# Output stage of a decoder layer: from channel rows to token rows, on one core

## The chip, the cores and the metric

The kernel runs on one core of a Trainium2 chip. The metric is the device time of one execution in microseconds, from runs of one program; lower is better. Engines are named as the profile names them: PE (TensorE, matmul; PEld is its weight load), DVE (VectorE), ACT (ScalarE), POOL (GpSimd), SP (SyncE), which issues most DMAs here. An ending q (SPq, PEq) is an engine's own queue of instructions. Values are fp32; the large products are made from split fp32r operands.

## The reference

One decoder layer over 1024 tokens with a model width of 1024: a half-step feed-forward block, a mixer (gated DeltaNet beside differential attention, merged by gates), a second feed-forward block, and a last RMSNorm. The change concerns the last line and the row of weights it needs:

```
def rms_norm(x, g, eps=RMS_EPS):                  # RMS_EPS = 1e-6
    y = x * rsqrt(mean(x * x, axis=-1) + eps)
    return y * g

x = x + 0.5 * swiglu_ffn(rms_norm(x, ffn2_norm), ffn2_w_gate, ffn2_w_up, ffn2_w_down)
return rms_norm(x, final_norm)                    # (1, 1024, 1024) float32
```

## The kernel before, in words

The stream x lives in SBUF as xT, transposed: 128 partitions by 8 chunks of channels by 1024 tokens, so that channel c sits on partition c mod 128 and the matmuls can contract over channels. Work is cut into phases (setup, feed-forward, five mixer phases, feed-forward, output). Each phase is one block with a program for each engine, ordered by semaphores that are waited for by hand; `end_phase` clears them and puts a barrier of all engines between phases (lines 86 to 90). There is no planner: the order on an engine is the order of its lines, and a wait holds up all that stands behind it on that engine.

**Setup** (`setup_phase`, line 119). SP loads four gain vectors into one tile, `gains` (lines 149 to 153), each spread over partitions in pieces of 4 bytes, and after them the rows of x, 128 tokens (512 KB) at a time into two slots (lines 154 to 157; a slot is loaded again once PE has transposed what it held). PE transposes each, DVE copies the result to xT (line 204). ACT's queue loads small mixer parameters at the same time (lines 601 to 613). The setup ends with a wait for all gains.

**Feed-forward** (`ffn_phase`, line 342). It ends with PE's last down product and `add_down` on DVE (line 472), which adds each chunk to xT.

**Output** (`output_phase`, line 281) uses the class `Norm` (line 209), as the other norms do, on the transposed x, where the sum over channels runs across partitions:
- ACT squares the eight chunks (line 227); DVE adds them in pairs (line 244).
- PE multiplies the four pair sums by a matrix of ones (line 251), which leaves the sum of squares of each token on all 128 partitions.
- ACT takes the root of 128 by 1024 (line 231), DVE its reciprocal (line 258), and then eight products of a chunk with its column of gains and the reciprocals (line 261).
- PE waits for all eight (`pe.wait_ge(norm.scaled, DC)`, line 311), then transposes token tile by token tile, two groups of four into four PSUM banks (line 317).
- DVE copies the even group of a tile (line 330), ACT the odd one (line 306), into one of two row tiles; SP stores it, 512 KB (line 337). From the third tile on both copies wait for the store that used the slot before.

Lines of other phases that the prediction uses for durations: 774 (a copy from PSUM on ACT), 1327 (the softmax's exp with a row sum), 1381 (a product with a pointer scalar and one input in PSUM), 1387 to 1398 (the one- and two-column operations behind the softmax), 766 (the root in the DeltaNet projection, with its table load), 616 and 618 (small exponentials in the setup).

Of the kernel before, what the change touches and what calls it, by code (L numbers as in the profile page):

```python
# [118 lines left out]
def setup_phase(core, a):  # L119

    nc = core.nc
    c = core
    per = core.ctx
    c.xT = c.sb(per, "xT", [P, DC, T])
    c.n_hi = c.sb(per, "n_hi", [P, DC, T], F32R)
    c.n_lo, c.n_raw = c.sb_shared(per, "n_lo", [P, DC, T])
    c.ident = c.sb(per, "ident", [P, P])
    c.ones = c.sb(per, "ones", [P, P])
    c.head_ones = c.sb(per, "head_ones", [P, P])
    c.ident2 = c.sb(per, "ident2", [P, CH])  # L130
    c.gains = c.sb(per, "gains", [P, 4, DC])
    c.eps = c.sb(per, "eps", [P, 2])

    gains_in = c.sem("gains_loaded")
    zeroed = c.sem("consts_zeroed")
    made = c.sem("consts_made")
    turned = c.sem("x_turned")
    taken = c.sem("x_taken")
    with ExitStack() as ctx:
        mixer_part = mixer_setup(core, a, ctx)  # L140
        xin = c.sb(ctx, "x_in", [P, 2, D_MODEL])
        xps = c.ps(ctx, "x_ps", [P, 4, HALF])
        slot_in = [c.sem("x_in_slot0"), c.sem("x_in_slot1")]
        block = ctx.enter_context(nc.Block())
        xrows = a["x"].rearrange("b (t p) d -> (b t) p d", p=P)

        @block.sync
        def _(sp):
            for i, name in enumerate(("ffn1_norm", "mix_norm", "ffn2_norm")):
                sp.dma_start(c.gains[:, i, :], a[name].rearrange("l (c p) -> p (l c)", p=P),  # L150
                             allow_slow_non_contiguous=True).then_inc(gains_in, 16)
            sp.dma_start(c.gains[:, 3, :], a["final_norm"].rearrange("(c p) -> p c", p=P),
                             allow_slow_non_contiguous=True).then_inc(gains_in, 16)
            for t in range(T // P):
                if t >= 2:
                    sp.wait_ge(turned, 2 * (t - 1))
                sp.dma_start(xin[:, t % 2, :], xrows[t]).then_inc(slot_in[t % 2], 16)
            sp.wait_ge(gains_in, 64)

        @block.gpsimd  # L160
        def _(pool):
            pool.memset(c.ident[:], 0.0).then_inc(zeroed, 1)
            pool.memset(c.ones[:], 1.0).then_inc(zeroed, 1)
            pool.memset(c.eps[:, 0:1], RMS_EPS).then_inc(zeroed, 1)
            pool.memset(c.eps[:, 1:2], SUBLN_EPS).then_inc(zeroed, 1)
            pool.memset(c.head_ones[:], 0.0).then_inc(zeroed, 1)
            pool.wait_ge(zeroed, 5)
            pool.affine_select(out=c.ident[:], in_=c.ident[:], compare_op=ALU.not_equal, fill=1.0, base=0,
                               pattern=[[-1, P]], channel_multiplier=1).then_inc(made, 1)
            mixer_part["gpsimd"](pool)  # L170

        @block.scalar
        def _(act):
            mixer_part["scalar"](act)

        @block.tensor
        def _(pe):
            pe.wait_ge(made, 1)
            for t in range(T // P):
                pe.wait_ge(slot_in[t % 2], 16 * (t // 2 + 1))  # L180
                for g in range(2):
                    k = 2 * t + g
                    if k >= 4:
                        pe.wait_ge(taken, k - 3)
                    for j in range(4):
                        d = 4 * g + j
                        last = pe.transpose(xps[:, k % 4, j * P:(j + 1) * P],
                                            xin[:, t % 2, d * P:(d + 1) * P], c.ident[:])
                    last.then_inc(turned, 1)
            mixer_part["tensor"](pe)  # L190

        @block.vector
        def _(dve):
            mixer_part["clear"](dve)
            dve.wait_ge(zeroed, 5)
            for h in range(2):
                dve.memset(c.head_ones[h * HD:(h + 1) * HD, h * HD:(h + 1) * HD], 1.0)
            dve.wait_ge(made, 1)
            dve.tensor_tensor(c.ident2[:], c.ident[:, 0:CH], c.ident[:, CH:P], ALU.add)
            for t in range(T // P):  # L200
                for g in range(2):
                    k = 2 * t + g
                    dve.wait_ge(turned, k + 1)
                    dve.tensor_copy(c.xT[:, 4 * g:4 * g + 4, t * P:(t + 1) * P],
                                    xps[:, k % 4, :].rearrange("p (j q) -> p j q", j=4)).then_inc(taken, 1)
            mixer_part["vector"](dve)


class Norm:
# [1 line left out]

    def __init__(self, core, which, rstd, ss, split=True):
        self.core, self.gain, self.rstd, self.ss, self.split = core, core.gains[:, which, :], rstd, ss, split
        self.squared = core.sem("squared")
        self.paired = core.sem("squares_paired")
        self.summed = core.sem("squares_summed")
        self.rooted = core.sem("rooted")
        self.inverted = core.sem("inverted")  # L220
        self.scaled = core.sem("scaled")
        self.hi_made = core.sem("n_hi_made")
        self.lo_made = [core.sem("n_lo_even_made"), core.sem("n_lo_odd_made")]
# [31 lines left out]
    def scale(self, dve):  # L255
# [4 lines left out]
        for k in range(DC):  # L260
            dve.scalar_tensor_tensor(out=c.n_raw[:, k, :], in0=c.xT[:, k, :], scalar=self.gain[:, k:k + 1],  # L261
                                     in1=self.rstd[:], op0=ALU.mult, op1=ALU.mult).then_inc(self.scaled, 1)
            if self.split and k % 2:
                self.lo_part(dve, k - 1)

    def lo_part(self, engine, k):
# [11 lines left out]
        pe.wait_ge(self.lo_made[k % 2], k // 2 + 1)  # L278


def output_phase(core, which, out):

    nc, c = core.nc, core
    turned = c.sem("y_turned")
    copied = c.sem("y_copied_even")
    copied_act = c.sem("y_copied_odd")
    with ExitStack() as ctx:
        rstd = c.sb(ctx, "rstd", [P, T])
        ss = c.ps(ctx, "ss", [P, NH, HALF])
        y = c.sb(ctx, "y", [P, 2, D_MODEL])  # L290
        yps = c.ps(ctx, "yps", [P, 4, HALF])
        slot_out = [c.sem("y_out0"), c.sem("y_out1")]
        norm = Norm(c, which, rstd, ss[:], split=False)
        block = ctx.enter_context(nc.Block())
        orow = out.rearrange("b (t p) d -> (b t) p d", p=P)

        @block.scalar
        def _(act):
            norm.squares(act)
            norm.root(act)  # L300
            for t in range(T // P):
                k = 2 * t + 1
                if t >= 2:
                    act.wait_ge(slot_out[t % 2], 16 * (t // 2))
                act.wait_ge(turned, k + 1)
                act.activation(y[:, t % 2, HALF:], yps[:, k % 4, :], ACT.Copy).then_inc(copied_act, 1)  # L306

        @block.tensor
        def _(pe):
            norm.sums(pe)  # L310
            pe.wait_ge(norm.scaled, DC)
            for t in range(T // P):
                for g in range(2):
                    k = 2 * t + g
                    past(pe, (copied, copied_act)[g], t - 1)
                    for j in range(4):
                        last = pe.transpose(yps[:, k % 4, j * P:(j + 1) * P],  # L317
                                            c.n_raw[:, 4 * g + j, t * P:(t + 1) * P], c.ident[:])
                    last.then_inc(turned, 1)

        @block.vector
        def _(dve):
            norm.pairs(dve)
            norm.scale(dve)
            for t in range(T // P):
                k = 2 * t
                if t >= 2:
                    dve.wait_ge(slot_out[t % 2], 16 * (t // 2))
                dve.wait_ge(turned, k + 1)
                dve.tensor_copy(y[:, t % 2, 0:HALF], yps[:, k % 4, :]).then_inc(copied, 1)  # L330

        @block.sync
        def _(sp):
            for t in range(T // P):
                sp.wait_ge(copied, t + 1)
                sp.wait_ge(copied_act, t + 1)  # L336
                sp.dma_start(orow[t], y[:, t % 2, :]).then_inc(slot_out[t % 2], 16)
            sp.wait_ge(slot_out[0], 16 * (T // P // 2))
            sp.wait_ge(slot_out[1], 16 * (T // P // 2))


def ffn_phase(core, which, w_gate, w_up, w_down):
# [1462 lines left out]
def build(nc, a, out):  # L1805
    with ExitStack() as ctx:
# [5 lines left out]
        mixer(core, a)  # L1812
        ffn_phase(core, 2, a["ffn2_w_gate"], a["ffn2_w_up"], a["ffn2_w_down"])
        core.end_phase()
        output_phase(core, 3, out)
        core.end_phase()


# [22 lines left out]
```

## Time and profile before

| | |
|---|---|
| median of 3 runs | 2977.3 us |
| lowest, highest | 2975.35, 2978.68 us |
| span of the profiled execution | 2974.8 us |
| its own time | not given by the profile; the span runs from its first to its last instruction |
| PE busy | 2670.5 us (90%), 17130 instructions |
| PE weight load | 2164.7 us (73%) |
| DVE busy | 1292.1 us (43%), 1443 instructions |
| ACT busy | 636.3 us (21%), 852 instructions |
| SP's DMA queue (q1) | 109.15 MB, 12.3% of 16 engines |
| mean granted clock of PE | 0.941 of full speed |

The page gives busy time over the whole span. The output stage lies inside the last fortieth of it, so its own state is read from the chain of waits, from the timeline and from windows cut around it. Times in such rows count from the start of the span. A row of the timeline gives start, length, engine, line, operation and tiles, the count of merged instructions, and in square brackets how long the engine sat idle before and what released it; a row without brackets followed at once. [...]

### The profile page before, as it was taken

The numbers are of one execution on the slowest core, as the hardware profiler recorded it, in microseconds if no ns is written. First come the engines' busy times: TensorE is split into PE (matmuls) and PEld (weight loads), VectorE is DVE, ScalarE is ACT, GpSimd is POOL, SyncE is SP. The second block draws the span as 40 slices with busy tenths as digits, with TensorE's granted clock in tenths as the row PEclk, the third lists the DMA queues.
The fourth block names the chain that finished last, engine by engine and source line by source line (L and its number), as shares of the span: only waits on it lengthen the run. The fifth ranks groups of instructions, "written<-read, shape, count | busy, mean of one in ns | idle before, by whom it ended". The sixth has DMA issues, their size and how long they took to land. (4 is left out here: it accounts for less than half of the span.)

```text
span 2974.8 us, 40256 instructions
## 1 busy us (share of the span) xinstructions
PE 2670.5 (90%) x17130; PEld 2164.7 (73%) x17130; DVE 1292.1 (43%) x1443; ACT 636.3 (21%) x852; POOL 72.8 (2%) x88
## 2 busy tenths in 40 slices
PE   4999999999789778777888698999969999999995
PEld 3888888888557677776666456888748888888874
DVE  6333333333478744443455542444363333333334
ACT  2111111111255211111333331111131111111111
POOL 2000000000010000000000000000010000000000
PEclk7999999999899888788999889999999999999997
DMA  3111111111110000001100001111011111111101
GB/s 85 50 57 50 49 49 44 48 42 49 29 29 28 1 3 3 3 3 37 29 22 1 15 15 57 46 47 49 28 57 50 47 45 49 42 56 45 48 27 57
DMA packets 167517, 110.97 MB, mean 37 GB/s; under 512 B 15336, under 2 KB 158696, under 8 KB 167400
## 3 DMA queue, kind: packets, MB, share of 16 engines
q1 hardware_dynamic: 160720, 109.15, 12.3%
q8 instruction: 102, 1.67, 0.2%
q10 hardware_dynamic: 6680, 0.03, 0.1%
q14 instruction: 15, 0.12, 0.0%
HBM read 104.97 MB, written 4.19 MB: 37 GB/s over the span
## 5 line engine op out<-in xcount | busy, mean ns | idle before, releaser
L472 DVE SCALAR_TENSOR_TENSOR xT<-ps_down,xT 128x1024 f32<-128x1024 f32 x176 | 215.6, 1225 | 247.5 <-PE ps_down L100 247.5
L455 DVE TENSOR_TENSOR w_lo<-w_raw,w_hi 128x1024 fp32r<-128x1024 f32 x132 | 163.6, 1253 | 352.5 <-ACT w_hi L409 352.5
L409 ACT ACTIVATE w_hi<-w_raw 128x1024 fp32r<-128x1024 f32 x132 | 136.9, 1053 | 745.1 <-PE ps_down L100 395.7
L96 PE MATMUL ps_gate<-n_hi,w_hi 128*128 128x512 f32 x704 | 220.8, 395 | 35.7 <-DVE n_lo_hi L269 25.1
L96 PE MATMUL ps_down<-h_hi,w_hi 128*128 128x512 f32 x704 | 218.2, 391 | 7.6 <-issue 7.6
L98 PE MATMUL ps_gate<-n_lo_hi,w_hi 128*128 128x512 f32 x704 | 218.5, 392 | 0.0
L100 PE MATMUL ps_gate<-n_hi,w_lo 128*128 128x512 f32 x704 | 218.1, 391 | 0.0
L98 PE MATMUL ps_down<-h_lo,w_hi 128*128 128x512 f32 x704 | 217.8, 391 | 0.0
L100 PE MATMUL ps_down<-h_hi,w_lo 128*128 128x512 f32 x704 | 217.6, 390 | 0.0
L98 PE MATMUL ps_up<-n_lo_hi,w_hi 128*128 128x512 f32 x704 | 216.7, 389 | 0.0
L96 PE MATMUL ps_up<-n_hi,w_hi 128*128 128x512 f32 x704 | 216.7, 389 | 0.0
L100 PE MATMUL ps_up<-n_hi,w_lo 128*128 128x512 f32 x704 | 216.7, 389 | 0.0
L461 DVE TENSOR_TENSOR h_raw<-silu_gate,ps_up 128x1024 f32<-128x1024 f32 x44 | 53.7, 1221 | 332.1 <-PE ps_up L100 332.1
L96 PEld LDWEIGHTS ps_gate<-n_hi,w_hi 128*128 128x128 f32 x704 | 132.0, 189 | 69.9 <-issue 24.7
L96 PEld LDWEIGHTS ps_down<-h_hi,w_hi 128*128 128x128 f32 x704 | 132.7, 189 | 35.8 <-issue 8.3
L98 PEld LDWEIGHTS ps_gate<-n_lo_hi,w_hi 128*128 128x128 f32 x704 | 133.5, 190 | 28.1
L100 PEld LDWEIGHTS ps_gate<-n_hi,w_lo 128*128 128x128 f32 x704 | 133.0, 189 | 28.0
L98 PEld LDWEIGHTS ps_down<-h_lo,w_hi 128*128 128x128 f32 x704 | 133.0, 189 | 27.8
L100 PEld LDWEIGHTS ps_down<-h_hi,w_lo 128*128 128x128 f32 x704 | 132.7, 188 | 27.7
L98 PEld LDWEIGHTS ps_up<-n_lo_hi,w_hi 128*128 128x128 f32 x704 | 132.1, 188 | 27.5
L96 PEld LDWEIGHTS ps_up<-n_hi,w_hi 128*128 128x128 f32 x704 | 132.1, 188 | 27.4
L100 PEld LDWEIGHTS ps_up<-n_hi,w_lo 128*128 128x128 f32 x704 | 132.1, 188 | 27.4
(303 smaller groups left out, 4104.9 us busy)
## 6 DMA issues: line engine op xcount, KB each, us to landing
w_raw<-in_ffn_w_gate SPq DMA_DIRECT2D x44, 512.0 KB, 3.7
w_raw<-in_ffn_w_up SPq DMA_DIRECT2D x44, 512.0 KB, 3.7
w_raw<-in_ffn_w_down SPq DMA_DIRECT2D x44, 512.0 KB, 3.6
w_raw<-in_w_in SPq DMA_DIRECT2D x44, 512.0 KB, 3.6
x_in<-in_x SPq DMA_DIRECT2D x8, 512.0 KB, 3.9
w_raw<-in_w_out SPq DMA_DIRECT2D x8, 512.0 KB, 3.5
y_out<-y SPq DMA_DIRECT2D x8, 512.0 KB, 2.6
w_raw<-in_w_branch_a SPq DMA_DIRECT2D x8, 256.0 KB, 3.0
```

The costliest lines, as they stand in the source:

```text
L96: pe.matmul(bank, w_hi, x_hi[:, h * HALF:(h + 1) * HALF], start=start, stop=False)
L98: pe.matmul(bank, w_hi, x_lo[:, h * HALF:(h + 1) * HALF], start=False, stop=False)
L100: last = pe.matmul(bank, w_lo, x_hi[:, h * HALF:(h + 1) * HALF], start=False, stop=stop)
L409: act.activation(ring.hi[:, slot(k)], ring.raw[:, slot(k)], ACT.Copy).then_inc(ring.hi_made, 1)
L455: dve.tensor_tensor(ring.lo[:, slot(k)], ring.raw[:, slot(k)], ring.hi[:, slot(k)].bitcast(F32), ALU.subtract).then_inc(ring.lo_made, 1)
L461: dve.tensor_tensor(h_raw[:, j, :], sg[:], ps_u[:].rearrange("p h t -> p (h t)"), ALU.mult).then_inc(h_made, 1)
L472: dve.scalar_tensor_tensor(out=c.xT[:, d, :], in0=ps_d[:, d % 2].rearrange("p h t -> p (h t)"), scalar=0.5, in1=c.xT[:, d, :], op0=ALU.mul ...
```

## The change

The output stage works on token rows. PE transposes xT as it stands, eight 128 by 128 pieces to a token tile, into one of four PSUM slots of 1024 columns (all eight banks). ACT squares a tile from PSUM and has the row sum accumulated in the same instruction, then takes the root of that one column; a one-column root at the head of the stage draws the table load there. DVE takes the reciprocal of the column and makes one product from PSUM: tile times column times a row tile of weights. SP loads the weight row, broadcast to 128 partitions, at the head of the stage, and stores each tile from one of four slots. The load of `final_norm` in the setup goes, `gains` keeps three columns, and `Norm` loses a flag that only the old stage used. The call becomes `output_phase(core, a, out)`.

```diff
--- before.py
+++ after.py
@@ -128,7 +128,7 @@
     c.ones = c.sb(per, "ones", [P, P])
     c.head_ones = c.sb(per, "head_ones", [P, P])
     c.ident2 = c.sb(per, "ident2", [P, CH])
-    c.gains = c.sb(per, "gains", [P, 4, DC])
+    c.gains = c.sb(per, "gains", [P, 3, DC])
     c.eps = c.sb(per, "eps", [P, 2])
 
     gains_in = c.sem("gains_loaded")
@@ -149,13 +149,11 @@
             for i, name in enumerate(("ffn1_norm", "mix_norm", "ffn2_norm")):
                 sp.dma_start(c.gains[:, i, :], a[name].rearrange("l (c p) -> p (l c)", p=P),
                              allow_slow_non_contiguous=True).then_inc(gains_in, 16)
-            sp.dma_start(c.gains[:, 3, :], a["final_norm"].rearrange("(c p) -> p c", p=P),
-                             allow_slow_non_contiguous=True).then_inc(gains_in, 16)
             for t in range(T // P):
                 if t >= 2:
                     sp.wait_ge(turned, 2 * (t - 1))
                 sp.dma_start(xin[:, t % 2, :], xrows[t]).then_inc(slot_in[t % 2], 16)
-            sp.wait_ge(gains_in, 64)
+            sp.wait_ge(gains_in, 48)
 
         @block.gpsimd
         def _(pool):
@@ -211,8 +209,8 @@
 
 
 
-    def __init__(self, core, which, rstd, ss, split=True):
-        self.core, self.gain, self.rstd, self.ss, self.split = core, core.gains[:, which, :], rstd, ss, split
+    def __init__(self, core, which, rstd, ss):
+        self.core, self.gain, self.rstd, self.ss = core, core.gains[:, which, :], rstd, ss
         self.squared = core.sem("squared")
         self.paired = core.sem("squares_paired")
         self.summed = core.sem("squares_summed")
@@ -260,7 +258,7 @@
         for k in range(DC):
             dve.scalar_tensor_tensor(out=c.n_raw[:, k, :], in0=c.xT[:, k, :], scalar=self.gain[:, k:k + 1],
                                      in1=self.rstd[:], op0=ALU.mult, op1=ALU.mult).then_inc(self.scaled, 1)
-            if self.split and k % 2:
+            if k % 2:
                 self.lo_part(dve, k - 1)
 
     def lo_part(self, engine, k):
@@ -278,65 +276,70 @@
         pe.wait_ge(self.lo_made[k % 2], k // 2 + 1)
 
 
-def output_phase(core, which, out):
+def output_phase(core, a, out):
 
     nc, c = core.nc, core
-    turned = c.sem("y_turned")
-    copied = c.sem("y_copied_even")
-    copied_act = c.sem("y_copied_odd")
+    NT = T // P
+    SLOTS = 4
     with ExitStack() as ctx:
-        rstd = c.sb(ctx, "rstd", [P, T])
-        ss = c.ps(ctx, "ss", [P, NH, HALF])
-        y = c.sb(ctx, "y", [P, 2, D_MODEL])
-        yps = c.ps(ctx, "yps", [P, 4, HALF])
-        slot_out = [c.sem("y_out0"), c.sem("y_out1")]
-        norm = Norm(c, which, rstd, ss[:], split=False)
+        gain = c.sb(ctx, "gain_rows", [P, D_MODEL])
+        y = c.sb(ctx, "y", [P, SLOTS, D_MODEL])
+        sq = c.sb(ctx, "y_squared", [P, D_MODEL])
+        ss = c.sb(ctx, "y_sums", [P, NT])
+        rstd = c.sb(ctx, "y_rstd", [P, NT])
+        yps = c.ps(ctx, "yps", [P, SLOTS, D_MODEL])
+        gain_in = c.sem("gain_in")
+        warm = c.sem("root_warm")
+        turned = c.sem("y_turned")
+        summed = c.sem("y_summed")
+        rooted = c.sem("y_rooted")
+        inverted = c.sem("y_inverted")
+        normed = c.sem("y_normed")
+        y_out = [c.sem(f"y_out{i}") for i in range(SLOTS)]
         block = ctx.enter_context(nc.Block())
         orow = out.rearrange("b (t p) d -> (b t) p d", p=P)
 
+        @block.tensor
+        def _(pe):
+            for t in range(NT):
+                past(pe, normed, t - SLOTS + 1)
+                for d in range(DC):
+                    last = pe.transpose(yps[:, t % SLOTS, d * P:(d + 1) * P], c.xT[:, d, t * P:(t + 1) * P],
+                                        c.ident[:])
+                last.then_inc(turned, 1)
+
         @block.scalar
         def _(act):
-            norm.squares(act)
-            norm.root(act)
-            for t in range(T // P):
-                k = 2 * t + 1
-                if t >= 2:
-                    act.wait_ge(slot_out[t % 2], 16 * (t // 2))
-                act.wait_ge(turned, k + 1)
-                act.activation(y[:, t % 2, HALF:], yps[:, k % 4, :], ACT.Copy).then_inc(copied_act, 1)
-
-        @block.tensor
-        def _(pe):
-            norm.sums(pe)
-            pe.wait_ge(norm.scaled, DC)
-            for t in range(T // P):
-                for g in range(2):
-                    k = 2 * t + g
-                    past(pe, (copied, copied_act)[g], t - 1)
-                    for j in range(4):
-                        last = pe.transpose(yps[:, k % 4, j * P:(j + 1) * P],
-                                            c.n_raw[:, 4 * g + j, t * P:(t + 1) * P], c.ident[:])
-                    last.then_inc(turned, 1)
+            act.activation(rstd[:, 0:1], c.eps[:, 0:1], ACT.Sqrt).then_inc(warm, 1)
+            act.wait_ge(warm, 1)
+            for t in range(NT):
+                act.wait_ge(turned, t + 1)
+                past(act, summed, t)
+                act.activation(sq[:], yps[:, t % SLOTS, :], ACT.Square, accum_out=ss[:, t:t + 1]).then_inc(summed, 1)
+                act.wait_ge(summed, t + 1)
+                act.activation(rstd[:, t:t + 1], ss[:, t:t + 1], ACT.Sqrt, scale=1.0 / D_MODEL,
+                               bias=c.eps[:, 0:1]).then_inc(rooted, 1)
 
         @block.vector
         def _(dve):
-            norm.pairs(dve)
-            norm.scale(dve)
-            for t in range(T // P):
-                k = 2 * t
-                if t >= 2:
-                    dve.wait_ge(slot_out[t % 2], 16 * (t // 2))
-                dve.wait_ge(turned, k + 1)
-                dve.tensor_copy(y[:, t % 2, 0:HALF], yps[:, k % 4, :]).then_inc(copied, 1)
+            dve.wait_ge(gain_in, 16)
+            for t in range(NT):
+                dve.wait_ge(rooted, t + 1)
+                dve.reciprocal(rstd[:, t:t + 1], rstd[:, t:t + 1]).then_inc(inverted, 1)
+                dve.wait_ge(inverted, t + 1)
+                if t >= SLOTS:
+                    dve.wait_ge(y_out[t % SLOTS], 16 * (t // SLOTS))
+                dve.scalar_tensor_tensor(out=y[:, t % SLOTS, :], in0=yps[:, t % SLOTS, :], scalar=rstd[:, t:t + 1],
+                                         in1=gain[:], op0=ALU.mult, op1=ALU.mult).then_inc(normed, 1)
 
         @block.sync
         def _(sp):
-            for t in range(T // P):
-                sp.wait_ge(copied, t + 1)
-                sp.wait_ge(copied_act, t + 1)
-                sp.dma_start(orow[t], y[:, t % 2, :]).then_inc(slot_out[t % 2], 16)
-            sp.wait_ge(slot_out[0], 16 * (T // P // 2))
-            sp.wait_ge(slot_out[1], 16 * (T // P // 2))
+            sp.dma_start(gain[:], a["final_norm"].unsqueeze(0).broadcast_to([P, D_MODEL])).then_inc(gain_in, 16)
+            for t in range(NT):
+                sp.wait_ge(normed, t + 1)
+                sp.dma_start(orow[t], y[:, t % SLOTS, :]).then_inc(y_out[t % SLOTS], 16)
+            for i in range(SLOTS):
+                sp.wait_ge(y_out[i], 16 * (NT // SLOTS))
 
 
 def ffn_phase(core, which, w_gate, w_up, w_down):
@@ -1812,7 +1815,7 @@
         mixer(core, a)
         ffn_phase(core, 2, a["ffn2_w_gate"], a["ffn2_w_up"], a["ffn2_w_down"])
         core.end_phase()
-        output_phase(core, 3, out)
+        output_phase(core, a, out)
         core.end_phase()
```

## Rows read from the trace of the kernel before

**Rows 1.** The page: its first line, and the queue of small packets.

```profile
span 2974.8 us, 40256 instructions
...
q10 hardware_dynamic: 6680, 0.03, 0.1%
```

**Rows 2.** The chain of waits, output stage: start us, us, what.

```profile
2926.50 2.01 ACT n_lo_raw L227 x2
...
2940.50 6.56 DVE rstd L258
...
2947.09 9.66 DVE n_lo_raw L261 x8
...
2956.79 3.69 PE yps L317 x16
...
2967.89 2.61 DMA y_out<-y
...
2970.52 0.69 DVE y L330
```

**Rows 3.** Timeline, the last addition of the feed-forward stage.

```profile
2924.43 1.23 DVE L472 SCALAR_TENSOR_TENSOR xT<-ps_down,xT 128x1024 f32<-128x1024 f32 x1 [1.49 <-PE ps_down L100]
```

**Rows 4.** Timeline, transposes of the setup, eight to a row.

```profile
14.68 1.09 PE L187 MATMUL x_ps<-ident,x_in 128*128 128x128 f32 x8 [2.13 <-DMA x_in<-in_x]
...
28.21 1.97 PE L187 MATMUL x_ps<-ident,x_in 128*128 128x128 f32 x8 [1.06 <-DMA x_in<-in_x]
```

**Rows 5.** Windows: us; PE, PEld, DVE, ACT, POOL busy; PEclk; DMA share; GB/s.

```profile
2924.00:2925.00 1.00, 0.39 (x2) 0.00 (x0) 0.57 (x1) 0.00 (x0) 0.00 (x0) 1.00 0.00 0
...
2927.00:2928.00 1.00, 0.00 (x0) 0.00 (x0) 0.00 (x0) 1.00 (x2) 0.00 (x0) 0.89 0.00 0
...
2956.00:2958.00 2.00, 1.21 (x6) 1.21 (x7) 0.79 (x2) 0.00 (x0) 0.00 (x0) 0.50 0.00 0
...
2962.00:2964.00 2.00, 1.98 (x17) 1.60 (x15) 0.87 (x2) 0.78 (x2) 0.00 (x0) 1.00 0.80 324
```

**Rows 6.** ACT: groups by form (busy us, mean ns), then timeline of a softmax.

```profile
L774 ACT ACTIVATE padded<-ps_proj 128x1024 f32<-128x1024 f32 x12 | 12.2, 1019 | 13.0 <-PE ps_proj L100 13.0
...
L231 ACT ACTIVATE rstd<-ss,eps 128x1024 f32<-128x1024 f32 x1 | 1.1, 1114 | 3.9 <-PE ss L251 3.9
...
L618 ACT ACTIVATE neg_a<-neg_a 16x1 f32<-16x1 f32 x1 | 0.2, 185 | 0.0
...
1640.45 1.14 ACT L1327 ACTIVATE scores<-scores,neg_max 128x1024 f32<-128x1024 f32 x1
1641.49 0.19 ACT L1327 ACTIVATION_READ_ACCUMULATOR scores<-scores,neg_max 128x1 f32 x1
1641.58 1.13 ACT L1327 ACTIVATE scores<-scores,neg_max 128x1024 f32<-128x1024 f32 x1
```

**Rows 7.** SP's waits (total, times, longest); landing times of the loads of x.

```profile
SPq L336 <- ACT y L306: 33.0, 1, 33.0
...
DMA to landing us min/median/max: 3.5/3.9/5.7
```

**Rows 8.** DVE: a product's group by form, then timeline in the attention stage.

```profile
L1381 DVE SCALAR_TENSOR_TENSOR scores<-bias,slopes,ps_scores 128x1024 f32<-128x1024 f32 x8 | 9.9, 1277 | 8.7 <-PE ps_turned L1246 8.7
...
1631.39 2.47 DVE L1381 SCALAR_TENSOR_TENSOR scores<-bias,slopes,ps_scores 128x1024 f32<-128x1024 f32 x2 [2.84 <-PE ps_turned L1246]
...
1645.34 0.16 DVE L1394 RECIPROCAL total<-total 128x2 f32<-128x2 f32 x1
1645.53 0.81 DVE L1396 TENSOR_SCALAR scores<-scores,total,neg_lam 128x1024 f32<-128x1024 f32 x1
```

**Rows 9.** Timeline of SP's queue in the setup.

```profile
2.55 1.21 SPq L152 DMA_DIRECT2D gains<-in_final_norm  x1
```

**Rows 10.** Timeline of ACT, a table load and its root.

```profile
868.37 1.28 ACT L766 ACT_TABLE_LOAD   x1
869.67 1.12 ACT L766 ACTIVATE root<-ps_sum,eps 128x1024 f32<-128x1024 f32 x1
```

## The prediction

> **What bounds the kernel now.** I read the page first: a span of 2974.8 us [rows 1], most of it PE's work in stages that the change does not touch. Such shares say nothing of the last stage, so I read the chain of waits next, which ended last there. From 2926.50 to the last copy at 2970.52 the stage is one serial chain [rows 2]: squares, pair sums, sums by matmul, root, reciprocal over 1024 columns (6.56), eight gain products (9.66), and only then, at 2956.79, transposition, copies and stores. The engines stand in a row here and each waits for the one before. The stage begins 0.84 us after the last add of the feed-forward stage (2925.66 to 2926.50), and its last copy ends at 2970.52 + 0.69 = 2971.21; behind it stand the last store and the closing, 2974.8 - 2971.21 = 3.6 us [rows 1 to 3]. In the store part two slots set the pace: a store lands 2.61 us after its issue, a copy of 0.69 follows, so two tiles take 3.3 us and the steps between, some 1.7 a tile [rows 2].
>
> **Part 1, the chain over channels goes.** All of 2926.50 to 2956.79, 30.3 us, is removed from the path, with the copies behind it. What takes its place is priced below from 2926.5 on, so the saving is the difference of the two ends of the last vector operation.
>
> **Part 2, the start.** PE can transpose as soon as the stage opens: x is complete and the identity is old. Eight transposes took 1.09 us at the full clock [rows 4], and 16 took 3.69 at the low one, 1.85 for eight [rows 2, 5]. PE enters at full clock (0.89 is the mean of 2927 to 2928 [rows 5]), so tile 0 is readable at about 2926.5 + 1.09 + 0.1 = 2927.7. ACT first loads the root table, 1.28, and does a one-column root. That root has a pointer bias: 128x1024 with one took 1114 ns and without one 1019, and a small one without took 185, so 0.28 [rows 6]. The first square starts at 2926.5 + 1.28 + 0.28 = 2928.1, behind tile 0. Before, that load lay under the sums; now it is open but cheap.
>
> The weight row comes by a DMA at the head of SP's queue in the stage. SP is in the stage at 2959.48 - 33.0 = 2926.45 [rows 7]. Nothing here shows a broadcast; the nearest is the load of x, the same 512 KB in rows of 4 KB into 128 partitions: 3.5 us at least, 3.9 median, 5.7 at most. Below it stands the store with 2.6. I take 3.5, since nothing else is in flight (the longer ones ran beside loads in small pieces): it lands at 2929.95, bounds 2929.05 and 2932.15. The vector engine waits for it ahead of all its work; behind that wait are all eight reciprocals, then PE from tile 4 (four slots) and the stores. Stores stand behind the load on SP for 0.33 us only, long before they are due. The squares run on meanwhile, up to the fourth slot.
>
> **Part 3, a tile on ACT.** Square with row sum, from PSUM: 1019 ns as the copy from PSUM; the read of the accumulator starts about 0.10 before its end and takes 0.19, as in the softmax (1640.45, 1641.49, 1641.58) [rows 6]. Sum ready at +1.11. Then the wait on its own result, 0.03 (no row on ACT; on the vector engine 1645.34 + 0.16 to 1645.53 [rows 8]), and the root, 0.28. The next square overlaps by 0.09: 1.33 a tile. Root of tile 0 at 2928.1 + 1.42 = 2929.5.
>
> **Part 4, a tile on the vector engine.** Reciprocal of one column: 0.158 for two columns; the product starts 0.20 after the reciprocal; product with pointer scalar and one input in PSUM 1.28; two such in a row took 2.47, so the next starts 1.19 after the first [rows 8]. 0.20 + 1.19 = 1.39, say 1.40 a tile. So the vector engine is the slowest of the chain, by little, and the end is: reciprocal 0 at 2929.98 (the weight row, 0.5 after root 0), + 7 x 1.40 + 1.48 = **2941.26**. Against 2971.21 that is 29.95 us less. If the weight row came at once, ACT would set it: 0.45 less. With 5.7 us of landing: 2.2 more.
>
> **Part 5, stores and slots.** A tile is stored every 1.40. A product from tile 4 on waits for the store issued 4 x 1.40 = 5.6 us less one product before, about 4.1, against 2.61 of landing: covered. With the queue busy the engines moved 324 GB/s at a share of 0.80 [rows 5], so 405 at a full one: 1.29 us for 512 KB, under 1.40. I leave the last landing and the closing at 3.6 us. Were these covers gone, the rival on stores has the price. The four slots of the transposes: tile t needs product t-4; PE (1.09) and ACT (1.33) then have 4.2 us. The work on PE and its weight loads lies beside.
>
> **Part 6, the setup.** One load in 4-byte pieces goes: 1.21 us of SP's queue ahead of the first load of x, from 2.55 on [rows 9]. PE's transposes in the setup wait for x [rows 4]. The stage is a chain of loads of x with two slots, so a shift of 1.21 should reach the end, but small loads from ACT's queue stay at their times and may eat part. Bounds 0 and 1.5; I take 0.9, nearer the issue time. The smaller gain tile moves the addresses behind it, at nothing: no row shows an address costing time, and its two bounds are the spread of the runs.
>
> **Sum.** 29.95 + 0.9 = 30.85. The profiled span is 2974.8; the execution's own time is not shown, and the median of the three runs, 2977.3, lies 2.5 above the span, which I leave as it is. 2977.3 - 30.85 = 2946.4 (a span of 2943.9).
>
> **Rivals.**
> A. *PE at the low clock for all tiles.* [...] A low clock for some tiles is in the forecast: tile 1 would come at 2929.5, covered by the weight row. Price if it stays: tile 7 at 2926.5 + 8 x 1.85 + 0.2 = 2941.5, + 1.11 + 0.31 + 0.20 + 1.28 + 0.05 = 2944.45, 3.2 more: 2949.6. Chance 0.08.
> B. *Stores set the pace.* If 324 GB/s is a ceiling and not the two slots' doing, a tile takes 1.62: first issue 2931.5, last landing 2931.5 + 7 x 1.62 + 2.61 = 2945.45 against 2943.9: 2948.0. Against it: the share of 0.80. Chance 0.10.
> C. *A table load at every change between square and root.* The change alternates them 8 times on ACT. The trace of before has a load ahead of each root and none ahead of a square, but nowhere does a square follow a root. Against: the squares that open this stage stand behind the silu of the feed-forward stage and begin without a load [rows 2], so they do not need the silu's loads; that they need none of the root's is not shown. Price by rows: a load takes 1.30 from its start to the next start [rows 10]; a tile takes 1.30 + 1.11 + 1.31 + 0.31 = 4.03, the last root is at 2928.1 + 8 x 4.03 = 2960.3, the last product ends at 2961.8, 9.4 less than before: 2977.3 - 9.4 - 0.9 = 2967.0. Chance 0.05.
> [...]
> D. *Slower: the broadcast goes in 4-byte pieces.* Place: the vector engine's first wait. The gain loads of before did so; 4 KB took 1.21 us of queue [rows 9], so 512 KB would take 128 x 1.21 = 155 us; by the share of the queue of small packets on the page, 0.1% of 2974.8 for 6680 packets [rows 1], 131072 packets take 58 us. The whole saving is gone when the row lands later than 3.5 + 30.85 = 34.4 us from issue; with 58 it lands at 2984.5, the time is 2977.3 + (2984.5 - 2929.95) - 30.85 = 3001, with 155 it is 3098. Against: source rows are contiguous over 4 KB as x's are, while the gains of before are spread over partitions. Chance 0.02.
> E. *The chain over channels was hidden.* Not possible by the chain of waits; that the text keeps one of its waits is not to be seen in the diff. Chance 0.01, 2977.
>
> **How the numbers follow.** Forecast 0.70, A 0.08, B 0.10, C 0.05, D 0.02, E 0.01, and 0.04 for something else between forecast and C. Predicted 2946.4. Its own bounds: down 0.45 (weight row), 0.6 (setup) and 1.95 for the spread of the runs (2977.3 - 2975.35), 3.0 together, 2943.4; up 2.2, 0.9 and 1.4: 2950.9. With A and B inside, the range is 2943.3 to 2951.5. A measurement tells 0.2% (6 us) from no change. Faster: 0.70 + 0.08 + 0.10 + 0.04 and 0.04 of C, 0.96; same: E, 0.01; slower: D, and 0.01 of C should a load cost 2.3 us and not 1.3, 0.03.
>
> **What would show it.** In the new profile: transposes from 2925.6 on (2926.5 less 0.9), one table load in the stage, squares near 1.02 with a 0.19 read, pitch of the products 1.40, the first product ended by the weight row and not by root 0, stores 2.6 to landing, no idle time of the vector engine before products from tile 4 on, 3.6 us from the last product to the end. Wrong: 16 loads (C), a pitch near 1.85 with clock 0.50 (A), a vector engine that waits for stores (B), a weight row over 6 us, or a setup that ends at the same time as before.

## The result, and the profile after

The changed kernel takes 2987.36 us (median of 13 runs, 2983.04 to 2990.72), the kernel before 2978.2 in the same comparison (13 runs, 2975.35 to 2982.36). The ratio is 1.003, 95% interval 1.0022 to 1.0039: slower by 0.3%, where 1% less was forecast. The profiled execution has a span of 2985.6 us, 10.8 more than before. Among the experiments below, one execution of the old stage with a wider tile took 14770 us, in the slow state, and is left out.

The chain of waits, output stage of the changed kernel (start us, us, what), answers to [rows 2]:

```profile
2967.45 3.29 DMA gain_rows<-in_final_norm
2970.74 0.02 issue
2970.77 0.18 DVE y_rstd L328
2970.94 0.03 issue
2970.97 1.28 DVE y L332
...
2980.69 1.28 DVE y L332
```

The stage opens at 2967.46 and its last product ends at 2980.69 + 1.28 = 2981.97: 14.51 us, where 44.71 stood before. The forecast stage was 2941.26 - 2926.5 = 14.8 us long; the change took 30.2 us out where 29.95 was forecast. But it opens 41 us later than before. Where from? The row of ACT with which each large stage begins, timeline of the changed kernel:

```profile
34.20 2.95 ACT L225 ACTIVATE n_lo_raw<-xT 128x1024 f32<-128x1024 f32 x3 [2.46 <-PEq L89]
...
810.14 5.79 ACT L225 ACTIVATE n_lo_raw<-xT 128x1024 f32<-128x1024 f32 x6 [28.12 <-PEq L89]
...
2191.81 4.84 ACT L225 ACTIVATE n_lo_raw<-xT 128x1024 f32<-128x1024 f32 x5 [16.24 <-PEq L89]
...
2967.46 1.28 ACT L313 ACT_TABLE_LOAD   x1 [28.09 <-PEq L89]
```

| stage | before | after |
|---|---|---|
| setup, to the first square | 34.43 | 34.20 |
| feed-forward 1 | 761.67 | 775.94 |
| mixer | 1370.22 | 1381.67 |
| feed-forward 2 | 760.18 | 775.65 |
| output, to the last product's or copy's end | 44.71 | 14.51 |

The starts before are 34.43, 796.10, 2166.32 and 2926.50; two of these rows, timeline of the kernel before:

```profile
796.10 4.84 ACT L227 ACTIVATE n_lo_raw<-xT 128x1024 f32<-128x1024 f32 x5 [27.11 <-PEq L89]
...
2166.32 3.90 ACT L227 ACTIVATE n_lo_raw<-xT 128x1024 f32<-128x1024 f32 x4 [16.41 <-PEq L89]
```

The three stages in the middle, which the change does not touch in any line of work, are 14.27 + 11.45 + 15.47 = 41.2 us longer; 41.2 - 30.2 - 0.2 = 10.8, the whole difference of the spans. The page shows on what engine: PE is busy for 2705.5 us against 2670.5.

The large products have this form. A chunk of weights is split into w_hi and w_lo, the normed x into n_hi and n_lo (the feed-forward's inner values into h_hi and h_lo). The function `three_pass` (from line 93 on) makes six matmuls of them, two halves of 512 tokens for each of three lines: w_hi with n_hi (L96), w_hi with n_lo (L98; the profile calls this tile n_lo_hi), w_lo with n_hi (L100). In the timeline each matmul has a weight load of its own (PEld, 128x128), which starts ahead of it and beside the matmul before: the first load of L98 starts at 2930.02 us, the first matmul of L98 at 2930.25, and the two of L96 take 2929.78 to 2930.41 (changed kernel, up product). n or h is the moving operand, the other input of the matmul's row, 128x512. The groups, page of the changed kernel (busy us, mean ns):

```profile
L98 PE MATMUL ps_up<-n_lo_hi,w_hi 128*128 128x512 f32 x704 | 221.3, 395 | 0.0
L96 PE MATMUL ps_up<-n_hi,w_hi 128*128 128x512 f32 x704 | 221.3, 395 | 0.0
L100 PE MATMUL ps_up<-n_hi,w_lo 128*128 128x512 f32 x704 | 221.3, 395 | 0.0
L96 PE MATMUL ps_down<-h_hi,w_hi 128*128 128x512 f32 x704 | 219.4, 393 | 7.5 <-issue 7.5
```

The first of them on the page of the kernel before:

```profile
L96 PE MATMUL ps_up<-n_hi,w_hi 128*128 128x512 f32 x704 | 216.7, 389 | 0.0
```

The up products had a mean of 389 ns each before and have 395 now; the down products, on the same weight tiles, 391 and 393. The timeline has it without the overlap of the modelled ends (changed kernel):

```profile
2926.98 0.63 PE L96 MATMUL ps_up<-n_hi,w_hi 128*128 128x512 f32 x2
2927.45 0.63 PE L98 MATMUL ps_up<-n_lo_hi,w_hi 128*128 128x512 f32 x2
2927.92 0.63 PE L100 MATMUL ps_up<-n_hi,w_lo 128*128 128x512 f32 x2
2928.38 0.63 PE L96 MATMUL ps_up<-n_hi,w_hi 128*128 128x512 f32 x2
...
2956.59 0.61 PE L100 MATMUL ps_down<-h_hi,w_lo 128*128 128x512 f32 x2
2957.04 0.62 PE L96 MATMUL ps_down<-h_hi,w_hi 128*128 128x512 f32 x2
2957.49 0.62 PE L98 MATMUL ps_down<-h_lo,w_hi 128*128 128x512 f32 x2
2957.95 0.61 PE L100 MATMUL ps_down<-h_hi,w_lo 128*128 128x512 f32 x2
```

Six up matmuls take 2928.38 - 2926.98 = 1.40 us from start to start, six down matmuls 2957.95 - 2956.59 = 1.36: 233.3 ns against 226.7 each. The granted clock is 1.00 in both stretches (PE busy 20.00 of 20.00 us in the window 2915 to 2935, 16.00 of 16.00 in 2948 to 2964), so it is not the clock. All products that move n_hi or n_lo are slow: 4224 in gate and up, 1152 in the projections of DeltaNet and attention, 192 in the branch norm and 768 in the merge. These are 6336, by 6.67 ns 42.2 us. (The expectations below count 6144, without the branch norm.)

PE's idle time does not grow: over the three stages in the middle it is busy for 2635.3 of 2892.1 us before and for 2683.1 of 2933.3 now. Each of these matmuls is 3% slower. That 42.2 lies so near to the 41.2 by which the stages are longer is in part chance: another part of the mixer is 3.6 us shorter (last section), so some 2.6 us more have no source named here.

### The profile page after: what moved, and what is told of

Same layout as the page of the kernel before. It is cut to its first block and busy times, and to the rows that moved or that the text cites. A ratio compares the mean times of both kernels' runs of the same rounds, so it can differ in the third digit from the quotient of the medians.

```text
span 2985.6 us, 40221 instructions
## 1 busy us (share of the span) xinstructions
PE 2705.5 (91%) x17114; PEld 2160.5 (72%) x17114; DVE 1275.7 (43%) x1438; ACT 633.0 (21%) x860; POOL 72.7 (2%) x88
## 5 line engine op out<-in xcount | busy, mean ns | idle before, releaser
L96 PE MATMUL ps_gate<-n_hi,w_hi 128*128 128x512 f32 x704 | 224.2, 399 | 37.3 <-DVE n_lo_hi L267 26.1
L96 PE MATMUL ps_down<-h_hi,w_hi 128*128 128x512 f32 x704 | 219.4, 393 | 7.5 <-issue 7.5
L100 PE MATMUL ps_gate<-n_hi,w_lo 128*128 128x512 f32 x704 | 222.1, 396 | 0.0
L98 PE MATMUL ps_gate<-n_lo_hi,w_hi 128*128 128x512 f32 x704 | 222.1, 396 | 0.0
L98 PE MATMUL ps_up<-n_lo_hi,w_hi 128*128 128x512 f32 x704 | 221.3, 395 | 0.0
L96 PE MATMUL ps_up<-n_hi,w_hi 128*128 128x512 f32 x704 | 221.3, 395 | 0.0
L100 PE MATMUL ps_up<-n_hi,w_lo 128*128 128x512 f32 x704 | 221.3, 395 | 0.0
L98 PE MATMUL ps_down<-h_lo,w_hi 128*128 128x512 f32 x704 | 218.8, 392 | 0.0
L100 PE MATMUL ps_down<-h_hi,w_lo 128*128 128x512 f32 x704 | 218.6, 392 | 0.0
L96 PEld LDWEIGHTS ps_gate<-n_hi,w_hi 128*128 128x128 f32 x704 | 131.5, 189 | 76.4 <-issue 24.7
L96 PEld LDWEIGHTS ps_down<-h_hi,w_hi 128*128 128x128 f32 x704 | 133.5, 190 | 36.5 <-issue 8.4
L98 PEld LDWEIGHTS ps_gate<-n_lo_hi,w_hi 128*128 128x128 f32 x704 | 132.5, 188 | 32.5
L100 PEld LDWEIGHTS ps_gate<-n_hi,w_lo 128*128 128x128 f32 x704 | 132.5, 188 | 32.5
L100 PEld LDWEIGHTS ps_up<-n_hi,w_lo 128*128 128x128 f32 x704 | 132.0, 187 | 32.3
L98 PEld LDWEIGHTS ps_up<-n_lo_hi,w_hi 128*128 128x128 f32 x704 | 132.0, 187 | 32.3
L96 PEld LDWEIGHTS ps_up<-n_hi,w_hi 128*128 128x128 f32 x704 | 132.0, 187 | 32.0
L98 PEld LDWEIGHTS ps_down<-h_lo,w_hi 128*128 128x128 f32 x704 | 133.3, 189 | 28.3
L100 PEld LDWEIGHTS ps_down<-h_hi,w_lo 128*128 128x128 f32 x704 | 133.3, 189 | 28.1
```

The lines of the kernel that those rows point to most:

```text
L96: pe.matmul(bank, w_hi, x_hi[:, h * HALF:(h + 1) * HALF], start=start, stop=False)
L98: pe.matmul(bank, w_hi, x_lo[:, h * HALF:(h + 1) * HALF], start=False, stop=False)
L100: last = pe.matmul(bank, w_lo, x_hi[:, h * HALF:(h + 1) * HALF], start=False, stop=stop)
```

## The experiments

Each time below is a median of four executions (ten for 128 bytes and for w_hi off, three for the old stage with a wider tile). Each ratio is to the kernel before in the same comparison, where that took 2976.7 to 2979.1 us; differences of 1 or 2 us between two experiments say nothing.

What n_hi and n_lo have to do with the change is not in its engines' programs. The gain tile went from 128 to 96 bytes a partition. Tiles are laid down one behind the other in the order of the kernel's calls: x, n_hi and n_lo ahead of the gain tile stayed, and all behind it (the weight ring, h_hi and h_lo, the mixer's tiles) moved down by 32 bytes. h and weights moved together, n and weights apart. That gave theory P: a matmul is slower when its weights and its moving operand lie at an unfavourable distance from each other. Against it stands theory Q: something else in the change slows PE.

### The tile restored

```diff
-    c.gains = c.sb(per, "gains", [P, 3, DC])
+    c.gains = c.sb(per, "gains", [P, 4, DC])
```

> The changed kernel, all of it, but the gain tile keeps four columns (128 bytes, the fourth unused), so every tile allocated behind it lies where it lay before the change. Theory P (placement: a matmul is slower when its weights and its moving operand start at places that differ by 32 bytes modulo 64): all products that move n_hi or n_lo return from 234 to 227 ns a matmul, the stages between setup and output take the 2892 us they took before, and the time is 2978.2 - 30.2 - 0.2 = 2947.8, 2945 to 2951. Theory Q (something else in the change slows PE: fewer DMAs in the setup, another set of semaphores, another program): 234 ns stay and the time stays near 2987.

Measured: 2947.57 us, ratio to before 0.9906 (0.9889 to 0.9922). By the same rows as above its feed-forward stages take 761.18 and 760.14, its mixer 1371.25; the up products are back (groups by form):

```profile
L96 PE MATMUL ps_up<-n_hi,w_hi 128*128 128x512 f32 x704 | 216.7, 389 | 0.0
```

Q falls. Every other part of the change is in this kernel, and 32 unused bytes are worth 40 us, four thirds of what the new output stage saves.

### The old stage with a wider tile

```diff
-    c.gains = c.sb(per, "gains", [P, 4, DC])
+    c.gains = c.sb(per, "gains", [P, 5, DC])
```

> The kernel before, nothing of the change, but the gain tile has five columns (160 bytes), so all behind it lies 32 bytes higher instead of 32 lower. Theory P: 6144 matmuls that move n_hi or n_lo take 6.7 ns more each, 41 us, 2978.2 + 41 = 3019, 3014 to 3024; the down products, whose two operands both move, stay at 227 ns. Theory Q: nothing, 2978.

Measured: 3019.46 us, ratio 1.0143 (1.0123 to 1.0164). The loss needs nothing of the change but the displacement, and either direction does.

### How far apart: 64, 128, 256 bytes

The changed kernel with `[P, 6, DC]`, `[P, 8, DC]` and `[P, 12, DC]`:

> The changed kernel with a gain tile of six columns (192 bytes): all behind it lies 64 bytes higher than before the change. Theory P with a period of 64 bytes: as with the tile restored, 2947.8 (2945 to 2951), 227 ns. With a period of 128 bytes or more the n products stay slow, near 234 ns, and the time near 2987. Theory Q: 2987.

> The changed kernel with a gain tile of eight columns, 256 bytes: all behind it lies 128 bytes higher than before the change. Theory P with a period of 128 bytes (64 was slow, 0 is not): 227 ns and 2947.6, 2945 to 2951. With a longer period: 233 ns in the n products, 2989. A shorter time than 2945 would mean that the old distance was not the best either.

> The changed kernel with a gain tile of 384 bytes: all behind it lies 256 bytes higher than before the change. In the kernel before every large product had its operands a multiple of 512 bytes apart; shifts of 32, 64 and 128 bytes were slow. Theory P with a period of 256: 227 ns and 2947.6, 2945 to 2951. With a period of 512: the n products near 233 ns and 2985 to 2990.

Measured: 2988.68 us for 64 bytes (ratio 1.0043, 1.0026 to 1.0059), 2985.46 for 128 (1.0029, 1.002 to 1.0039), 2947.12 for 256 (0.99, 0.9883 to 0.9916). My guesses of a period of 64 and of 128 were both wrong; the displacements seen to be fast are 0 and 256 bytes. Steps of 512 change nothing: within a stage the weights step by 512 bytes from chunk to chunk and the moving operand by 4096, and by 2048 from half to half, and in the kernel before the gap has a median of 227 ns in each large product. No profile shows a tile's address; that the operands lay a multiple of 512 bytes apart in the kernel before, as the last of these texts has it, was assumed, and no run shows it. The displacements count from the old places. Median gap from the start of one up matmul to the next, first and second of a pair, and the time (from the records of starts in each trace):

| displacement, bytes | n products: first, second ns | down products | us |
|---|---|---|---|
| 0 | 227, 227 | 227 | 2947.57 |
| -32 (the change) | 233, 234 | 227 | 2987.36 |
| +32 (old stage) | 232, 235 | 227 | 3019.46 |
| +64 | 233, 233 | 227 | 2988.68 |
| +128 | 238, 229 | 227 | 2985.46 |
| +256 | 227, 227 | 227 | 2947.12 |

The pair's mean is 233 to 233.5 wherever the products lose time: the pattern shifts, the sum does not. No displacement tried gave a faster n product than the old place. The time of +256 cannot be told from that of 0 (ratios 0.99 and 0.9906, with overlapping intervals).

### Distance or place

All 32 bytes off, the tile restored:

```diff
+    c.sb(per, "gap", [P, 8])
     c.xT = c.sb(per, "xT", [P, DC, T])
```

> The changed kernel with the tile restored and a gap of 32 bytes ahead of everything, so that every tile lies 32 bytes off, n and the weights alike. Theory P (only the distance between a matmul's moving operand and the weights modulo 128 bytes counts): 227 ns everywhere and 2947.6 as with the tile restored, 2945 to 2951. Theory R (each operand has to start at a multiple of 128 bytes): all large products slow, 6144 + some 2900 matmuls by 6.7 ns, 60 us, 3008.

Measured: 2948.39 us, ratio 0.9905 (0.9888 to 0.9922), 227 ns everywhere. R falls: with all operands 32 bytes off, each operand's own place has changed and nothing is slower; the distance between them matters.

The other pair of operands displaced, with n and weights in place:

```diff
         self.lo = core.sb(ctx, "w_lo", [P, depth, DC, P], F32R)
+        core.sb(ctx, "gap", [P, 8])
```

> The changed kernel with the tile restored and a gap of 32 bytes behind w_lo: the weights and n stay, what follows them (h_hi and h_lo in the feed-forward stages, merged_hi and merged_lo in the merge) lies 32 bytes off. Theory P: gate, up and projections stay at 227 ns, the down products (2112) and those of the merge's output (384) go to 233.5: 16.5 us over the tile restored, 2964, 2961 to 2968. A theory in which the writes of ACT and DVE, or a tile's own place, do the harm says that gate and up become slow too, as they did with the gap ahead of w_lo: near 2991.

Measured: 2965.4 us, ratio 0.9955 (0.9938 to 0.9971). Groups by form of this kernel, now with the roles exchanged:

```profile
L96 PE MATMUL ps_down<-h_hi,w_hi 128*128 128x512 f32 x704 | 224.0, 399 | 7.6 <-issue 7.6
...
L96 PE MATMUL ps_up<-n_hi,w_hi 128*128 128x512 f32 x704 | 217.1, 390 | 0.0
```

ACT and DVE write the displaced h here while gate and up run, and these stay fast. The changed kernel has a stretch that says the same: from 2929.20 to 2937.00 the up products run at 233.3 ns each while DVE, ACT and POOL are busy for 0.00 us and the DMA share is 0.00. No other engine is needed for the loss. What is left is PE's own work: in these 7.80 us its matmuls were busy for 7.75 and its weight loads for 5.88, beside them.

### Which two reads

> The changed kernel with the tile restored and a gap of 32 bytes between w_hi and w_lo, so w_lo and what follows (h_hi and h_lo among it) lie 32 bytes off, w_hi and n do not. It tells which pair of reads disturb each other. Theory P1 (the load of the next weights disturbs the matmul that runs meanwhile): in gate and up the second matmul of L98 and the first of L100 are slow, so the mean of both lines rises by 3.3 ns and L96 stays; in down (h off, w_hi not) both of L96, the first of L98 and the second of L100. Theory P2 (a matmul's own weights and its moving operand must agree): gate and up slow in L100 alone, both, by 6.7 ns; down slow in L96 and L98, fast in L100. Both give a third of 6144 and two thirds of some 2900 matmuls: 14 + 13 = 27 us over the restored tile, 2975, 2969 to 2980. Theory Q: no change against the restored tile.

> The changed kernel with the tile restored; in the two feed-forward stages w_hi alone lies 32 bytes off (a gap of 32 bytes ahead of it and one of 480 behind it, so w_lo and h lie 512 higher). Theory P1 (the next load disturbs the running matmul): of each six matmuls the four during which a w_hi is loaded are slow, L96 both, L98 first, L100 second; L98 second and L100 first stay at 227. Theory P2 (own weights and moving operand): L96 and L98 slow, L100 fast. Both: 4224 matmuls by 6.7 ns, 28 us over the tile restored, 2976, 2971 to 2981. If gate and up come out slow in all six, as with the gap ahead of w_lo, P1 is not the whole rule.

```diff
 # gap ahead of w_lo
         self.hi = core.sb(ctx, "w_hi", [P, depth, DC, P], F32R)
+        core.sb(ctx, "gap", [P, 8])
         self.lo = core.sb(ctx, "w_lo", [P, depth, DC, P], F32R)
 # w_hi off, feed-forward stages alone
+        core.sb(ctx, "gap", [P, 8])
         self.hi = core.sb(ctx, "w_hi", [P, depth, DC, P], F32R)
+        core.sb(ctx, "gap", [P, 120])
```

In their terms, P1 says that a running matmul is slowed by the load of the next weights, P2 that it is slowed by the place of its own weights. Measured: 2991.64 us (ratio 1.0049, 1.0032 to 1.0066) and 2982.26 (1.0013, 1.0004 to 1.0023), so 44 and 35 us over the restored tile and not 27 and 28. Median gaps in ns in the order of the six matmuls of a chunk; the last column is the median from the first start of one six to that of the next, so the rows need not add up to it:

| | L96 | L96 | L98 | L98 | L100 | L100 | all six |
|---|---|---|---|---|---|---|---|
| in place, all products | 227 | 227 | 227 | 227 | 227 | 227 | 1360 |
| gap ahead of w_lo, down | 233 | 234 | 231 | 227 | 227 | 235 | 1387 |
| gap ahead of w_lo, up | 233 | 231 | 232 | 235 | 231 | 231 | 1395 |
| w_hi off, gate, up and down | 231 | 229 | 235 | 232 | 231 | 235 | 1393 |

The down products of the first kernel are what P1 says, to the matmul: only the two during which an agreeing w_lo is loaded are fast. P2 would have made both of L98 slow and both of L100 fast. But its gate and up products, and all of the second kernel, are slow in every one of the six, which neither predicts: four agreeing loads in six (first kernel) or two (second) do not save their matmuls there. Shown is that the distance between moving operand and weights counts, and for the down products of the first kernel that it is the distance to the weights loaded during the matmul. Which load meets which matmul elsewhere, and why a misplaced one also costs its neighbours, stays open.

Operands in place do not rule out such gaps either. In the kernel before, behind sums that start every 429 ns (line 1474), the first products of the branch norm (from 1722.7 us on, granted clock 1.00) start 235, 233, 236, 224, 231, 236, 228, 233 and 231 ns apart and then settle to 226 and 227. Why they settle no run tested.

### A version to beat both

Weight row loaded during the last feed-forward stage, root table drawn at its end, x loaded ahead of the three gain vectors:

```diff
+        row = core.sb(ctx, "gain_row", [P, D_MODEL + P])   # first try: D_MODEL and a tile of 32
+        core.gain_row, core.root_first = row[:, 0:D_MODEL], row[:, D_MODEL:D_MODEL + 1]
...
+                act.activation(core.root_first, c.eps[:, 0:1], ACT.Sqrt)
...
+                sp.dma_start(c.gain_row, row.unsqueeze(0).broadcast_to([P, D_MODEL])).then_inc(row_in, 16)
```

> A version to beat both: the tile restored, the weight row loaded and the root table drawn during the last feed-forward stage, and the loads of x issued ahead of the three gain vectors in the setup. By the timeline of the changed kernel the first reciprocal stands 3.3 us behind the opening of the stage because of the weight row; without it the chain is transposes 1.2, square and its sum 1.11, root 0.3, so 2.65: 0.65 us less. The setup should give the queue time of three gain loads, 1.7 us at most, 0.5 by what the removal of the fourth gave. 2947.6 - 0.65 - 0.5 to 1.7 = 2945.9, 2943 to 2949; theory Q has no say in it.

Measured: 2958.44 us, ratio 0.9935 (0.9919 to 0.9952), 11 more than the restored tile. I had fallen into the same hole: 4096 + 128 bytes ahead of the ring of the last stage, 128 modulo 512. In its trace, last feed-forward stage:

```profile
L96 PE MATMUL ps_up<-n_hi,w_hi 128*128 128x512 f32 x352 | 110.7, 395 | 0.0
```

> The version with the weight row and the root table drawn early and x loaded first, now with the row tile 4608 bytes wide, 9 times 512, and not 4224: the weights of the last feed-forward stage keep their distance to n modulo 512. Theory P: the last feed-forward stage returns to 227 ns (it had 238 and 229 in turn) and the time falls from 2958.4 by 12.5 to some 2945.5; by the parts, 2947.6 less 0.85 in the output stage and 1.3 to 2.3 in the setup: 2945.0, 2942 to 2948. Theory Q, that the early loads themselves slowed that stage: it stays near 2958.

Measured: 2944.44 us, ratio 0.9887 (0.9871 to 0.9904), and the same group:

```profile
L96 PE MATMUL ps_up<-n_hi,w_hi 128*128 128x512 f32 x352 | 108.4, 389 | 0.0
```

This is the lowest median, though its interval overlaps that of the restored tile; the trace shows what it has over it: the first square of feed-forward 1 at 31.09 and not 33.57 us, and 0.4 in the output stage (PE's first transpose at 2924.97, last product ended at 2937.80 + 1.28 = 2939.08: 14.1, against 14.5).

## Why the prediction was wrong

**The step that failed** stands in part 6: "The smaller gain tile moves the addresses behind it, at nothing: no row shows an address costing time". The trace before had next to nothing to show: within a stage the operands of the large products change their distance by multiples of 512 bytes alone, from chunk to chunk and from half to half, and all ran at a median of 227 ns. The one other case in the same form is 48 small products of the DeltaNet projection, with weights of 16 columns laid 64 bytes apart. The last of them, from 840.89 us on, start 238, 234, 235, 229, 233 and 233 ns apart; but they are few and stand behind waits, and the large products right behind them, with their operands in place, start with gaps like these too (from 842.29 us on 236, 228, 233 and 230 ns, then 226 or 227), so they prove nothing alone. I saw the displacement and priced it by the absence of evidence, although the term is multiplied by every matmul that it touches: at 3% of each, 40 us between the restored tile and the change. The two-sided bound that I gave it, the spread of the runs, was not a bound on a price per matmul. The slower rival that I chose, a broadcast in small pieces (D), had its place in the stage that the change rewrites; the loss came from stages whose programs it leaves as they are.

The rest held. The restored tile is the change without the displacement and took 2947.57 us against the forecast 2946.4; against the kernel before in its own comparison (2976.7) that is 29.1 us less, where 30.85 was forecast. (The lower end of the range, 2943.3, is 0.1 off its own sum, 2946.4 - 3.0 = 2943.4.)

- **Part 1, output stage.** Forecast 29.95 us less, measured 30.2.
- **Part 2, start.** The weight row landed 3.29 us after its issue (3.5 taken) and released the first reciprocal; root 0 stood 0.3 ahead (timeline of the changed kernel: 2970.14 + 0.30 against 2970.77).
- **Part 3, ACT.** Square 1.00 to 1.02, read of the sum 0.19, root 0.29 to 0.30, pitch 1.33:

```profile
2970.34 1.00 ACT L318 ACTIVATE y_squared<-yps 128x1024 f32<-128x1024 f32 x1
2971.24 0.19 ACT L318 ACTIVATION_READ_ACCUMULATOR y_squared<-yps 128x1 f32 x1
2971.46 0.29 ACT L320 ACTIVATE y_rstd<-y_sums,eps 128x1 f32<-128x1 f32 x1
2971.66 1.00 ACT L318 ACTIVATE y_squared<-yps 128x1024 f32<-128x1024 f32 x1
```

- **Part 4, DVE.** Product 1.28, reciprocal 0.15, pitch 1.39 (1.40 taken), no idle time from the first product to the last:

```profile
2976.34 0.15 DVE L328 RECIPROCAL y_rstd<-y_rstd 128x1 f32<-128x1 f32 x1
2976.53 1.28 DVE L332 SCALAR_TENSOR_TENSOR y<-yps,y_rstd,gain_rows 128x1024 f32<-128x1024 f32 x1
2977.73 0.15 DVE L328 RECIPROCAL y_rstd<-y_rstd 128x1 f32<-128x1 f32 x1
```

- **Part 5, stores.** 2.7 us to landing, 391 GB/s at a share of 0.97 in 2975 to 2977: never waited for, but near a full share (by estimate 391 / 0.97 = 403 GB/s). Rival B took 324 GB/s for the ceiling, and the engines moved more.
- **Part 6, setup.** 0.9 taken; the first square came 0.23 earlier in the changed kernel, 0.86 with the tile restored. Over all nine kernels with this setup it is 0.2 to 0.9, so 0.9 was the upper end. What kept the rest was not looked into.
- **Rival A**: the clock did not fall here (granted 1.00 from 2967.50 to 2971.20, after PE had sat idle for 2.14 us). The length of the pause does not settle it: with the tile restored PE sat idle for 2.13 us, and the granted clock was 0.70 in 2927 to 2928 and 0.50 in 2928 to 2930, where six tiles took 7.34 us; in the kernel before, after 5.43 us, it was 0.50 in 2928 to 2929. The two stages took 14.51 us (changed kernel) and 14.57 (tile restored) to the last product's end, so a low clock for some tiles was covered, as forecast. In the changed kernel the first 32 transposes took 3.68 us, 0.92 a tile, less than the 1.09 that I took:

```profile
2967.50 3.68 PE L307 MATMUL yps<-ident,xT 128*128 128x128 f32 x32 [2.14 <-PEq L89]
```

- **Rival C**: one table load in the stage, at 2967.46; a square runs behind a root without one (root 2971.46 + 0.29, the next square at 2971.66). No load stands between the eight squares and the roots among them. The share of C in "slower" needed a load of 2.3 us, which no run shows; this one took 1.28.
- **Rivals D, E**: the row landed in 3.29 us; the chain over channels is gone.

## What to carry to other kernels

When a change alters the size of one tile, list which tiles move with it and which stay, and for every matmul that repeats look at the distance between its weights and its moving operand: here the old distance and 256 bytes more were fast (227 ns), and 32 less or 32, 64 and 128 more cost 3% of each matmul (233.3 ns). A stage is not untouched because its program is; compare the mean of one instruction, by group, in stages that should be equal before reading anything into the total. Keep the pad when a tile shrinks, and check again after each new tile laid ahead of a weight ring.

## What the runs showed of the hardware

In these runs the time of a matmul depended on how far its weights lie from its moving operand. With a 512-column moving operand at the granted clock 1.00 a matmul started every 226.7 ns with the operands in place (kernel before, tile restored) or 256 bytes farther apart, and every 233.1 to 233.4 ns on average with a displacement of 32, 64, 128 or -32 bytes (means of the up products). Both operands displaced together by 32 bytes were as fast as before, 226.7 ns and 2948.39 us. The displacement by 32 bytes alone moved the time by 40 us (2987.36 against 2947.57), and no other engine is needed for the loss: from 2929.20 to 2937.00 us of the changed kernel the matmuls start every 233.3 ns while DVE, ACT and POOL are busy for 0.00 us at a DMA share of 0.00. What makes a displaced pair slower inside PE is not shown.

One stage varies for a reason that the runs do not give. In the changed kernel the chunked DeltaNet stage is 3.6 us shorter than before, by SP's wait for its end (before 377.2 us), though no line of it changed:

```profile
SPq L915 <- PEq L915: 373.6, 1, 373.6
```

With the tile restored the same wait is 376.9 again, which looks like the displacement. But in the kernel with the gap ahead of w_lo, where the tiles of this stage lie at their old places, it is 373.7. So the displacement is not shown to be its cause, which stays open.
